# Three seven-product pairs instead of two in each gate/up chunk of a two-layer trunk kernel

## The reference

```python
def swiglu_ffn(x, norm_pre, w_gate, w_up, w_down, norm_post):
    h = rms_norm(x, norm_pre)
    a = jax.nn.silu(jnp.einsum('bsd,df->bsf', h, w_gate)) * jnp.einsum('bsd,df->bsf', h, w_up)
    y = jnp.einsum('bsf,fd->bsd', a, w_down)
    return x + rms_norm(y, norm_post)
```

## Time and profile before

| | us |
|---|---|
| median of 3 runs (1962.79 to 1964.47) | 1964.45 |
| span of the profiled execution, first to last instruction | 1962.1 |
| TensorE busy | 1945.9 (99%) |
| TensorE weight loads busy | 1653.3 (84%) |
| VectorE busy | 1570.1 (80%) |
| ScalarE busy | 1114.0 (57%) |
| GpSimd busy | 201.8 (10%) |

### The profile page before, as it was taken

The page is one execution under the profiler, slowest core; times in us unless marked ns, Lnnn a source line. Parts: engine busy times, 40 slices in busy tenths (PEclk is TensorE's granted clock), DMA queues, the critical chain, the costliest instruction groups (busy, mean ns, idle before and its releaser), DMA issues.

```text
span 1962.1 us, 26334 instructions
## 1 busy us (share of the span) xinstructions
PE 1945.9 (99%) x9646; PEld 1653.3 (84%) x9646; DVE 1570.1 (80%) x2016; ACT 1114.0 (57%) x1396; POOL 201.8 (10%) x127
## 2 busy tenths in 40 slices
PE   9999999999999999999999999999999999999998
PEld 7898888888888888888899988788888888888886
DVE  5755478888888868788699996688888888688787
ACT  6544465555555545555778875465555555455454
POOL 1000000000000000000489950000000000000000
PEclk9999999999999999999999999999999999999999
DMA  9645557666766766666355545557666667766564
GB/s 330 235 144 190 182 172 236 214 229 218 241 225 223 239 222 209 211 193 207 138 193 178 184 143 194 164 195 248 225 218 212 222 228 243 241 203 214 191 213 154
DMA packets 138011, 408.13 MB, mean 208 GB/s; under 512 B 15330, under 2 KB 38498, under 8 KB 137378
## 3 DMA queue, kind: packets, MB, share of 16 engines
q1 hardware_dynamic: 135796, 396.84, 61.7%
q0 software_dynamic: 2096, 9.70, 1.3%
HBM read 392.84 MB, written 13.63 MB: 207 GB/s over the span
## 4 chain that ended last, share of the span: by engine, by line
PE 97%; DVE 1%; ACT 1%; issue 0%; DMA 0%; POOL 0%; SPq 0%; DVEq 0%; ACTq 0%; POOLq 0%
PE acc L1705 68%; PE acc L1896 5%; PE acc L1897 5%; PE acc L1895 5%; PE acc L1716 4%; PE acc L1718 4%; PE acc L1717 4%; DMA raw<-in_units 0%; PE acc L2057 0%; PE acc L1757 0%; DVE x L1136 0%; PE acc L1755 0%; PE acc L2035 0%; ACT junk L698 0%; DVE acc L1119 0%
## 5 line engine op out<-in xcount | busy, mean ns | idle before, releaser
L681 ACT ACTIVATE w_hi<-raw 128x1024 fp32r<-128x1024 f32 x480 | 502.3, 1058 | 488.9 <-PE acc L1705 276.8
L1100 DVE TENSOR_TENSOR w_lo<-raw,w_hi 128x1024 fp32r<-128x1024 f32 x412 | 493.8, 1219 | 147.8 <-ACT w_hi L681 146.2
L1102 DVE SCALAR_TENSOR_TENSOR w_lo<-raw,vecs,w_hi 128x1024 fp32r<-128x1024 f32 x222 | 282.6, 1282 | 161.6 <-ACT w_hi L681 161.0
L681 ACT ACTIVATE w_hi<-raw,vecs 128x1024 fp32r<-128x1024 f32 x222 | 254.7, 1152 | 250.8 <-PE acc L1705 175.2
L1705 PE MATMUL acc<-w_hi,xT_hi 128*128 128x512 f32 x1240 | 383.4, 390 | 2.3 <-DVE w_lo L1102 1.7
L1705 PE MATMUL acc<-w_lo,xT_hi 128*128 128x512 f32 x1240 | 382.0, 389 | 0.0
L1705 PE MATMUL acc<-w_hi,xT_lo 128*128 128x512 f32 x1240 | 381.8, 389 | 0.0
L1705 PEld LDWEIGHTS acc<-w_hi,xT_hi 128*128 128x128 f32 x1240 | 231.7, 188 | 52.4 <-issue 3.5
L1705 PEld LDWEIGHTS acc<-w_lo,xT_hi 128*128 128x128 f32 x1240 | 232.7, 188 | 48.6
L1705 PEld LDWEIGHTS acc<-w_hi,xT_lo 128*128 128x128 f32 x1240 | 232.7, 188 | 48.5
L1716 PE MATMUL acc<-xT_hi,w_hi 128*128 128x256 f32 x640 | 181.2, 283 | 0.0
(11 more groups left out here) (276 smaller groups left out, 2697.9 us busy)
## 6 DMA issues: line engine op xcount, KB each, us to landing
raw<-in_units SPq DMA_DIRECT2D x702, 512.0 KB, 4.2
hid_turned_blocks<-tok SPq DMA_DIRECT2D x44, 256.0 KB, 4.1
tok<-hid_turned_blocks SPq DMA_DIRECT2D x176, 64.0 KB, 2.1
gpost<-in_post POOLq DMA_DIRECT2D x4, 1024.0 KB, 8.0
x<-in_x POOLq DMA_DIRECT2D x4, 512.0 KB, 8.2
c_raw<-in_consts POOLq DMA_DIRECT2D x4, 512.0 KB, 7.3
out<-x SPq DMA_DIRECT2D x8, 256.0 KB, 2.8
xT_raw<-in_xT SPq DMA_DIRECT2D x3, 512.0 KB, 7.2
```

Of the source, the lines that this page charges most:

```text
L681: nc.scalar.activation(w_hi[:, s, :], raw[:, s, :], ACT.Copy, scale=scale).then_inc(hi_ready, 1)
L1100: ins = nc.vector.tensor_tensor(w_lo[:, s, :], raw[:, s, :], w_hi[:, s, :], ALU.subtract)
L1102: ins = nc.vector.scalar_tensor_tensor(w_lo[:, s, :], raw[:, s, :], vecs[:, gain:gain + 1], w_hi[:, s, :], ALU.mult, ALU.subtract)
```

## The change

`FAST_QUADS = (1, 2)`, two pairs in each of chunks 1 to 9 at units 4 and 8, becomes `FAST_AT = (4, 7, 10)`, three pairs at units 4, 7 and 10, with the plain units 6 and 9 between them. Pairs may now span two quads, which `next_unit` resolves. The input's sums get three groups instead of two. `keep_first` and `add_parts` move behind the splits of units 14 and 15. `hidden`, `turn_hidden` and `lo_hid` keep their places between the same units' splits, counted by unit: after the first pair's `lo_sums`, after unit 6, and after unit 11. One wait of TensorE ahead of the down stage goes (`hT_lo_ready` for 20 blocks; each quad there still waits for its own). The program of SP is unchanged but for line numbers.

```diff
-FAST_QUADS = (1, 2)
+FAST_AT = (4, 7, 10)
...
+def next_unit(q, s):
+
+    return (q, s + 1) if s < 3 else (q + 1, 0)
...
-            xs_hi = mrow("xs_hi", [P, 2, BANK], F32R)
-            xs_lo = mrow("xs_lo", [P, 2, BANK], F32R)
-            mrow("between", [P, 2, BANK])
+            xs_hi = mrow("xs_hi", [P, 3, BANK], F32R)
+            xs_lo = mrow("xs_lo", [P, 3, BANK], F32R)
...
+        def gate_tiles(x):
+
+            return x[:, 7:KT, :].rearrange("p (a k) c -> p a (k c)", k=3)[:, :, SEQ:3 * SEQ]
...
-                def split_fast(q, n, raw_sum):
+                def split_pair(q, s, n, raw_sum):
 
                     act.wait_ge(raw_corner_ready, n)
-                    split(q, 0)
-                    split(q, 1)
+                    split(q, s)
+                    split(*next_unit(q, s))
                     act.wait_ge(raw_sum_ready, n)
                     if n > 1:
                         act.wait_ge(sums_used, n - 1)
                     nc.scalar.activation(sum_hi[:], raw_sum, ACT.Copy).then_inc(sum_hi_ready, 1)
-                    split(q, 2)
-                    split(q, 3)
...
+                    hi_hid(i - 1, 0)
+                    hi_hid(i - 1, 1)
+                    split_quad(q + 3, gain, 4)
+                    if i in FAST_CHUNKS:
+                        keep_first(gate_sum(layer, i, len(FAST_AT) - 1), par if i % 2 == 0 else 1 - par, parts, i)
...
-                join_rows(gate_raw_sum, first_tiles(xT_hi, 8, 2), first_tiles(xT_lo, 8, 2), 2)
-                sum_rows(gate_raw_sum, 2, (1 + len(SUM_BATCHES)) * (e // 2) + 1)
+                join_rows(gate_raw_sum, gate_tiles(xT_hi), gate_tiles(xT_lo), 3)
+                sum_rows(gate_raw_sum, 3, (1 + len(SUM_BATCHES)) * (e // 2) + 1)
...
+                    u = 4
+                    while u < 12:
+                        if fast and u in FAST_AT:
+                            n = FAST_AT.index(u)
+                            if n:
+                                sum_units(q + u // 4, u % 4, gate_sum(layer, i, n), gate_raw_sum)
+                            split_pair(q + u // 4, u % 4, gate_sum(layer, i, n), gate_raw_sum, gate_sum_lo[:])
+                            u += 2
+                        else:
+                            split(q + u // 4, u % 4)
+                            u += 1
+                        if u == 6 and i - 1 in FAST_CHUNKS:
+                            dve.wait_ge(closed, closed_count(layer, i - 1))
+                            hidden(i - 1, 0)
+                            hidden(i - 1, 1)
+                        if u == 7:
+                            turn_hidden(i - 1, 0)
+                            turn_hidden(i - 1, 1)
                     lo_hid(i - 1, 0)
                     lo_hid(i - 1, 1)
                     split(q + 3, 0, gain + 4)
                     split(q + 3, 1, gain + 5)
-                    if fast:
-                        add_parts(gate_sum(layer, i, fast[-1]), closing(layer, i - 1), z, parts)
                     split(q + 3, 2, gain + 6)
                     split(q + 3, 3, gain + 7)
+                    if fast:
+                        add_parts(gate_sum(layer, i, len(FAST_AT) - 1), closing(layer, i - 1), z, parts)
...
-                pe.wait_ge(hT_lo_ready, 22 * layer + 20)
```

More of the change, by code:

```diff
@@ L152, in parted, with gate_sum @@
     return 8 * ((b - 1) // 2) + by_tile_halves(t, c) + 1
[L155 to L157 removed]
+def gate_sum(layer, i, n):
+    return LAYER_SUMS * layer + len(FAST_AT) * (i - 1) + n + 1
+def next_unit(q, s):
+    return (q, s + 1) if s < 3 else (q + 1, 0)
 def down_sum(layer, j, c):
@@ L873, in ffn @@
                 rows = (1 + len(SUM_BATCHES)) * layer
-                hi_rows(rows + 1, xs_hi[:], gate_raw_sum[:, 0:2 * BANK].rearrange("p (a c) -> p a c", c=BANK))
+                hi_rows(rows + 1, xs_hi[:], gate_raw_sum[:, 0:3 * BANK].rearrange("p (a c) -> p a c", c=BANK))
                 for i in range(1, FFC):
-                    split_quad(i * 4 + q0, gain, 0)
+                    q = i * 4 + q0
+                    for s in range(4):
+                        split(q, s, gain + s)
                     silu(i - 1, 0)
                     silu(i - 1, 1)
[L879 to L887, removed]
-                        else:
[L889 to L892, removed]
+                    u = 4
+                    while u < 12:
+                        if i in FAST_CHUNKS and u in FAST_AT:
+                            split_pair(q + u // 4, u % 4, gate_sum(layer, i, FAST_AT.index(u)), gate_raw_sum)
+                            u += 2
+                        else:
+                            split(q + u // 4, u % 4)
[5 more added lines that the diff above has]
+                        keep_first(gate_sum(layer, i, len(FAST_AT) - 1), par if i % 2 == 0 else 1 - par, parts, i)
                 qd = q0 + Q_FF
@@ L898, in ffn @@
                         if c in FAST_DOWN[j]:
-                            split_fast(q, down_sum(layer, j, c), down_raw_sum[:])
+                            split_pair(q, 0, down_sum(layer, j, c), down_raw_sum[:])
+                            split(q, 2)
+                            split(q, 3)
                         elif c == FFC - 1:
@@ L1337, in lo_hid, with sum_units @@
                                             ALU.subtract).then_inc(hT_lo_ready, 1)
-                def sum_units(q, n, raw_sum):
+                def sum_units(q, s, n, raw_sum):
                     if n > 1:
                         dve.wait_ge(sum_lo_ready, n - 1)
-                    for s in range(2):
-                        dve.wait_ge(raw_landed[s], landings(q, s) * 16)
-                    b11, b12, b21, b22 = [raw[:, s, h * BANK:(h + 1) * BANK] for s in range(2) for h in range(2)]
+                    units = ((q, s), next_unit(q, s))
+                    for unit in units:
+                        dve.wait_ge(raw_landed[unit[1]], landings(*unit) * 16)
+                    b11, b12, b21, b22 = [raw[:, unit[1], h * BANK:(h + 1) * BANK] for unit in units for h in range(2)]
                     t3, t2, t4 = [raw_sum[:, n * BANK:(n + 1) * BANK] for n in range(3)]
@@ L1451, in ffn @@
                         if c in FAST_DOWN[j]:
-                            split_fast(q, down_sum(layer, j, c), down_raw_sum[:], down_sum_lo[:])
+                            split_pair(q, 0, down_sum(layer, j, c), down_raw_sum[:], down_sum_lo[:])
+                            split(q, 2)
+                            split(q, 3)
                         elif j == 0 and c < len(SUM_BATCHES):
@@ L1503, in ffn @@
                                 dve.wait_ge(rows_lo_ready, rows + 1 + len(SUM_BATCHES))
-                            sum_units(q + 1, down_sum(layer, j, c + 1), down_raw_sum[:])
+                            sum_units(q + 1, 0, down_sum(layer, j, c + 1), down_raw_sum[:])
             ffn(0, Q_F0, V_PRE["f0"], 1, 1)
```

74 lines of the change are left out of this document (30 added, 44 removed).

## The result

The changed kernel takes **1969.67 us** (median, 1966.04 to 1970.88), the kernel before 1963.55 (1962.69 to 1964.88) on the same chip: a ratio of **1.0027 [1.0018, 1.0036]**, slower by some 6 us. Forecast was +15.0. The direction was right, the size was over twice too large; the range given, 1962 to 1994, was wide enough to hold the time.

What follows compares the result with a forecast made beforehand. TensorE, never waiting inside a chunk, was taken as the bound. 18 x (-0.68 + 0.44 + 0.96) + 2.0 = 15.0 us, added to 1964.45, gave 1979.4; range 1962 to 1994.

Steps and rivals of the forecast that it cites:

- TensorE's saving: Three matmuls fewer in each of 18 chunks save 0.68 a chunk, 12.24 in all, if TensorE never waits.
- VectorE's walk: VectorE's work followed in order through a chunk: unit 12 is ready 0.44 late, making a chunk 41.92 against 42.16.
- The wait for unit 11: The third `sum_units` waits 0.96 for unit 11's load, and this goes into each chunk in full.
- w = L - 3.74: At the third `sum_units`, the wait w is the time L of unit 11's load less 3.74.
- L = 4.7: Time assumed for unit 11's load, the median of nine such loads in layer 0 before the change.
- The row with 5.3: A profiled load with fetches right behind it took 5.3; it backed the slow-load rival, 1990 to 2006, chance 0.18.
- The Trainium skill's figure: 2.0 us plus bytes at 436 GB/s, 3.2 for unit 11's 512 KB load: no wait, the change worth -2.3 us.
- load lands in time: Rival: unit 11's load takes under 3.74, so no wait at the third `sum_units`; -2.3, 1962.1; chance 0.14.
- Chunk 1: In chunk 1 of each layer VectorE is further behind than elsewhere, by 1.44 and 0.57, 2.0 in all.
- just in time: The second pair's remainder is ready for TensorE at 20.90 in a chunk, wanted at 21.08.
- What costs nothing: `keep_first` and `add_parts` behind split 15, ScalarE's third rounding and the third group of input sums stay hidden.

Runs made afterwards that it cites:

- e1: The changed kernel run again without any edit, for a second profile; 1969.02 us, ratio 1.0026 to the kernel before.
- e4: The changed kernel without its third pair, so with pairs at units 4 and 7 only; 1967.14 us, ratio 1.0017 to the kernel before.
- e2: The changed kernel with `lo_hid` moved from before the split of unit 12 to behind it; 1965.59 us, ratio 1.0009 to the kernel before.
- f2: The changed kernel with three of the eight fetches issued ahead of unit 11's load; 1997.83 us, ratio 1.0176 to the kernel before.
- f3: The changed kernel with all eight fetches issued ahead of unit 11's load; 2058.09 us, ratio 1.0491 to the kernel before.
- e3: The changed kernel without the stores and fetches of inner chunks 0 to 9; 1966.94 us, ratio 1.0015 to the kernel before.
- f4: The kernel of f1 with pairs at units 4 and 7 only; 1965.71 us, ratio 1.0010 to the kernel before.
- g1: The kernel of g2 with e2's edit besides; 1968.23 us, ratio 1.0026 to the kernel before.
- g2: The changed kernel with chunk 1 of each layer on two pairs, its inner tile's turn, copies and splits later; 1970.99 us, ratio 1.0034 to the kernel before.
- h1: The changed kernel with the subtraction for the inner tile's low parts moved from VectorE to GpSimd for chunks 0 to 9; ratio 1.0063 to the kernel before.
- f1: The changed kernel with the inner tile's turn, stores, fetches and splits moved later in the chunk; 1987.53 us, ratio 1.0115 to the kernel before.

## Why the prediction was right or wrong

- **TensorE's saving, 0.68 a chunk**: right. The pace stayed 0.2267, and the gaps and the saving add up to the span in the profiles of after, e1 and e4.
- **VectorE's walk, 0.44 late at unit 12, a loop of 41.92**: right within 0.1 (0.42, and 41.96 to 42.0), though 0.08 of it sits at unit 10. It is the main reason why the change gains next to nothing: of 0.68 a chunk it leaves 0.20. Its cause, the place of `lo_hid`, is shown by e2.
- **The wait for unit 11, 0.96 a chunk, 17.3 in all**: this is the step that failed. The rule w = L - 3.74 is right within 0.1 (waits of 1.16 and 1.33 at loads of 5.0 and 5.1; the slope by f2 and f3). The value L = 4.7 was not: it measured 3.7 in the median, and the waits came to 3.0 in the profile and 5.8 in e1. I took the median of the same load before, "the same load with the same traffic at a little other distance", but the traffic was not the same. Before, the stores were issued 1.7 ahead of it and unit 10's load 2.3 ahead, and that was still under way for 1.5 us; now the stores are 4.4 ahead and unit 10's load 5.0 ahead, and it has landed. Unit 10's load before, and under it after (SP's timeline, and from issue to landing):

```profile
434.68 0.33 SPq L465 DMA_DIRECT2D raw<-in_units  x1
DMA to landing us min/median/max: 3.8/3.8/3.8
436.67 0.33 SPq L473 DMA_DIRECT2D raw<-in_units  x1
DMA to landing us min/median/max: 3.9/3.9/3.9
```

  Which of the two neighbours made most of the 1.0, no run separates: in e3, without any copy, unit 11's load alone takes 3.2 to 3.4, and one issued at 424.15, 2.5 behind another that is still under way, takes 4.1. The row with 5.3 that I read as the price of fetches behind was no guide to it, for it too was issued 1.1 behind another load.
- The Trainium skill's figure (DMA: Bandwidth & Descriptors, section "Anatomy of one DMA — SWDGE (gpsimd) path"), an estimate of 3.2, which I set aside, made "load lands in time" the case to expect. The trace sides with that outcome; the load took 3.7 beside its neighbours and 3.2 to 3.4 only without the copies (e3).
- **"Load lands in time"**, with a chance of 0.14, was the rival nearest to the truth for fifteen or sixteen of eighteen chunks. That the whole came out slower all the same, as forecast, is owed to chunk 1 and to the two or three late loads with their aftermath, not to the 0.96 in each chunk: in this the direction was right by luck.
- **Chunk 1, 2.0 in all**: the size was about right (2.3), the place was not. I carried VectorE's lateness to unit 12 and missed that the pair at unit 7 has less in hand: I had called it "just in time" for its sums in a regular chunk (0.18), and didn't walk it for chunk 1. e4 and f4 show that it comes from the new order and not from the third pair or the wider input sums.
- **What costs nothing**: `add_parts` and `keep_first` behind unit 15, ScalarE's third rounding and the sums of input all stayed hidden; no gap stands at any of their places.
- **Missing altogether**: the stretches at half clock after a longer stall, 1.2 to 1.6 each (two of them in e1, none in the first profile), and the spread that they and the late loads give to the runs.

In sum, 18 chunks give back 12.2. In the first profile they lose 6.1 ahead of unit 12, 2.3 ahead of unit 7, 2.4 in small gaps at unit 10 and 3.0 with the two late loads, and 0.9 lies outside: 2.5. In e1, a usual run, it is 5.4, 2.3, 1.5 and 9.6 with three late loads and their aftermath: 6.6.

What stays open in part: unit 11 lands 1.5 to 3 late in just those chunks, with and without the copies (e3). The place moved in g1 and g2, and before the change chunk 3 had 6.2. In each of these cases a 16 KB packet of the `instruction` queue started during the load (see e3; before, 2.4 after the issue). Why such a packet should cost a load that much is not shown, and nothing tried here took it away.

## What to carry to other kernels

When an edit makes one load's landing decide, price that load from rows with the traffic that it will have, and state how long it may take: here the whole forecast hung on whether 3.74 is over or under it. The traffic includes the load ahead of it, if that is still under way. A mean room of 5.8 us on an engine says nothing about where the next wait falls; walk each point of the order, in the special first round as well as in the regular one. Once the engine is full (40.4 of 42.0), moving work or copies only moves the wait, so count what each move puts late before making it.

## What the runs showed that I had not expected

- TensorE's granted clock fell from 2.4 to 1.2 GHz for some 4 us, in f2 and f3 at times 7, after most of its stalls of 2 us and more (e1, e2, f2, f3), and 0.20 was lost on each matmul.
- Every late landing of unit 11's load in seven profiles (17 of 17) had a 16 KB packet of the `instruction` queue start while it was under way; of the 105 in time, none had one start within 3.3 of the issue.
- GpSimd slows VectorE: 1.98 and 2.32 for a split instead of 1.27 while both run, and GpSimd's own 128x512 subtraction took 2.42 and 2.28, and 1.30 where it started ahead of the split (h1).
- A load of 512 KB takes 3.2 to 3.4 with quiet queues (e3), 3.7 with eight 64 KB fetches behind (after), 3.6 to 4.7 with three ahead (f2) and 3.8 to 4.4 with all eight ahead (f3). With other loads close around as well it took 4.0 to 6.3 right behind all eight (f1, chunks 1 to 8).
